# Retention's values computed in the value stage, for all heads at once and kept in DRAM, instead of in a unit of each pair

## What is computed

```
h = rmsnorm(x)
qA,kA,vA | qR,kR,vR,gR | gateA,gateB = split(h @ w_in)
y_A = dilated attention(qA, kA, vA) @ w_a          # 24 heads of 64, three dilation groups of 8 heads
ret = retention(qR, kR, vR)                        # 4 heads, keys 128 wide, values 256 wide
y_B = (silu(gR) * ret * rsqrt(mean(ret^2)))  @ w_b
x = x + (sigmoid(gateA) * y_A + sigmoid(gateB) * y_B) @ w_o
x = x + relu(rmsnorm(x) @ w_up)^2 @ w_down
```

## Time and profile before

| | us |
|---|---|
| median of three runs | 1916.44 (1916.28 to 1916.62) |
| profiled execution, its own time | 1916.38 |
| its span, first to last instruction | 1914.6 |
| TensorE busy | 1907.6 |
| VectorE busy | 1132.0 |
| ScalarE busy | 772.1 |
| GpSimd busy | 89.3 |

### The profile page before, as it was taken

How to read it: one execution, slowest core, us unless ns; L and a number is a source line. 1 busy time by engine, 2 the same in 40 slices (tenths; PEclk the granted TensorE clock), 3 DMA queues, 4 the chain that set the end, 5 groups by cost and what they waited for, 6 DMA issues and landing times.

```text
span 1914.6 us, 23788 instructions
## 1 busy us (share of the span) xinstructions
PE 1907.6 (100%) x9664; PEld 1605.9 (84%) x9664; DVE 1132.0 (59%) x1785; ACT 772.1 (40%) x1197; POOL 89.3 (5%) x72
## 2 busy tenths in 40 slices
PE   9999999999999999999999999999999999999999
PEld 8888888888888888888888888888888888888888
DVE  5567786966456545445635576858755565445354
ACT  7344536463223323223352536454632333223232
POOL 0011110200000000000001110201000000000000
PEclk9999999999999999999999999999999999999999
DMA  4532323224333332332324233223243333323322
GB/s 146 170 94 78 93 84 90 83 67 143 100 110 99 99 96 92 94 105 88 110 96 147 89 88 89 83 77 95 67 154 107 99 92 100 98 88 98 100 88 88
DMA packets 211228, 190.83 MB, mean 100 GB/s; under 512 B 12848, under 2 KB 199984, under 8 KB 210352
## 3 DMA queue, kind: packets, MB, share of 16 engines
q1 hardware_dynamic: 210688, 188.97, 32.2%
q10 hardware_dynamic: 432, 0.35, 0.1%
HBM read 182.87 MB, written 6.43 MB: 99 GB/s over the span
## 4 chain that ended last, share of the span: by engine, by line
PE 98%; ACT 1%; DVE 0%; issue 0%; POOL 0%; DVEq 0%; ACTq 0%; POOLq 0%
PE pj L1474 27%; PE pj L1476 27%; PE pj L1475 27%; PE pj L1682 2%; PE pj L1683 2%; PE pj L1684 2%; PE sc L1581 1%; PE pt L1581 1%; PE sc L1609 1%; PE pt L1589 1%; PE yo L1609 1%; PE sc L1589 1%; PE sc L1539 1%; PE pt L1541 1%; PE sc L1541 1%; PE pt L1539 1%
## 5 line engine op out<-in xcount | busy, mean ns | idle before, releaser
L1474 PE MATMUL pj<-h_hi,w_hi 128*128 128x512 f32 x1408 | 553.4, 393 | 0.0
L1476 PE MATMUL pj<-h_hi,w_lo 128*128 128x512 f32 x1408 | 548.4, 389 | 0.0
L1475 PE MATMUL pj<-h_lo,w_hi 128*128 128x512 f32 x1408 | 548.2, 389 | 0.0
L538 ACT CAST w_hi<-w_raw 128x1024 fp32r<-128x1024 f32 x324 | 325.6, 1049 | 341.0 <-PE pj L1476 247.5
L900 DVE TENSOR_TENSOR w_lo<-w_raw,w_hi 128x1024 fp32r<-128x1024 f32 x327 | 395.3, 1248 | 98.1 <-ACT w_hi L538 96.7
L1474 PEld LDWEIGHTS pj<-h_hi,w_hi 128*128 128x128 f32 x1408 | 264.3, 188 | 56.9 <-issue 1.9
L1476 PEld LDWEIGHTS pj<-h_hi,w_lo 128*128 128x128 f32 x1408 | 264.3, 188 | 55.9
L1475 PEld LDWEIGHTS pj<-h_lo,w_hi 128*128 128x128 f32 x1408 | 264.4, 188 | 53.9 <-issue 0.5
L1474 PE MATMUL pj<-z_hi,w_hi 128*128 128x512 f32 (+1 forms) x656 | 252.0, 384 | 0.0
L1476 PE MATMUL pj<-z_hi,w_lo 128*128 128x512 f32 (+1 forms) x656 | 251.8, 384 | 0.0
L1475 PE MATMUL pj<-z_lo,w_hi 128*128 128x512 f32 (+1 forms) x656 | 251.8, 384 | 0.0
(11 more groups left out here) (262 smaller groups left out, 2338.1 us busy)
## 6 DMA issues: line engine op xcount, KB each, us to landing
w_raw<-in_w_in SPq DMA_DIRECT2D x151, 512.0 KB, 4.5
w_raw<-in_w_up SPq DMA_DIRECT2D x64, 512.0 KB, 4.6
w_raw<-in_w_down SPq DMA_DIRECT2D x64, 512.0 KB, 4.2
w_raw<-in_w_b SPq DMA_DIRECT2D x16, 512.0 KB, 3.8
w_raw<-in_w_o SPq DMA_DIRECT2D x16, 512.0 KB, 4.0
x_scratch<-x SPq DMA_DIRECT2D x2, 2048.0 KB, 10.2
x<-row_scratch SPq DMA_DIRECT2D x16, 256.0 KB, 3.8
w_raw<-in_w_a SPq DMA_DIRECT2D x8, 512.0 KB, 3.4
```

Of the source, the lines that this page charges most:

```text
L538: nc.scalar.copy(w_hi[s][:, c], raw[:, c]).then_inc(hi_done, 1)
L1474: nc.tensor.matmul(out, w_hi[s][:, wc], acts[0], start=first, stop=False)
L1475: nc.tensor.matmul(out, w_hi[s][:, wc], acts[1], start=False, stop=False)
L1476: return nc.tensor.matmul(out, w_lo[s][:, wc], acts[0], start=False, stop=last)
```

## The change

Retention's values leave the pairs. The value stage has five groups: vA group 0, then two groups with the 512 columns of two retention heads each (`VR_AT = (1, 2)`, with h in normal token order), then vA groups 1 and 2. ScalarE writes their high part (`vR_high`) and VectorE their low part into `vT_hi`, `vT_lo`, `vT_last`; SyncE writes these to DRAM (`vR_away`) and reads one head back in each pair (`vR_back`). A pair has five units (0 to 2, 3, and the gate as unit 4). The small matmuls keep their places relative to the unit before them, so that more of them now stand inside units of the next pair (`pair_rest`). The order on ScalarE and VectorE is rewritten for this. The gates of quarter 1 are split: A1 goes ahead of the first w_b unit (`GATES`), with a second buffer `sA1`.

```diff
-    V_U, P_U, G_U, O_U, M_U = 2, 6, 4, 2, 8
+    V_U, P_U, G_U, O_U, M_U = 2, 5, 4, 2, 8
+    VG = 5
+    VR_AT = (1, 2)
+    V_GROUP = (0, None, None, 1, 2)
+    GATES = [("A", 0), ("B", 0), ("A", 1), ("Z", 0), ("Y", 0), ("B", 1), ("Z", 1), ("Y", 1)]
+    GATES += [(k, p) for p in (2, 3) for k in "ABZY"]
...
+                def vR_away(r):
+                    sp.wait_ge(v_out, (l * VG + VR_AT[r] + 2) * TB)
+                    h2 = slice(2 * r, 2 * r + 2)
+                    sp.dma_start(vr_hi_scratch[:, h2], vT_hi[:].bitcast(F32).rearrange("p e b c -> p e (b c)")).then_inc(vr_sent, 16)
...
+                def vR_back(i):
+                    J = l * PAIRS + i
+                    sp.wait_ge(vr_sent, (l + 1) * 96)
+                    sp.wait_ge(rstd_all_done, 2 * l + 1)
+                    sp.wait_ge(ret_mm, 2 * J + 2)
+                    sp.dma_start(vR_hi[:].bitcast(F32).rearrange("p b c -> p (b c)"), vr_hi_scratch[:, i]).then_inc(vr_in, 16)
...
                 value_weights(2)
+                vR_away(0)
+                value_weights(3)
+                vR_away(1)
+                value_weights(4)
                 x_out()
...
+                def vR_high(r):
+                    act.wait_ge(rstd_done, l + 1)
+                    if r == 1:
+                        act.wait_ge(vr_sent, (2 * l + 1) * 48)
+                    for b in range(TB - 1):
+                        act.wait_ge(v_done, (l * VG + VR_AT[r]) * (TB - 1) + b + 1)
+                        nc.scalar.activation(vT_hi[:, :, b, :],
...
                         if g == 0:
                             pe.wait_ge(h_ready, l * 2 * KT + k + 1)
-                        elif g == 1:
+                        elif g == 3:
                             pe.wait_ge(res_done, l * KT + k + 1)
...
-                        for o in range(2):
-                            pe.wait_ge(bank_free[o], l * LQ + i * P_U + 5 + BANK_CREDIT)
+                        pe.wait_ge(vr_in, (J + 1) * 48)
...
                 g0 = l * LU + G0
                 last = l * PAIRS + PAIRS - 1
-                gate(0, 0, 0)
+                gate("B", 0, 0)
                 split_z(range(0, 6))
-                gate(0, 0, 1)
+                gate("B", 0, 1)
                 ret_inverse(last)
-                lo(g0 + 2, 0)
-                gate(0, 1, 0)
+                lo(g0 + 3, 1)
                 ret_scale(PAIRS - 1, 0)
                 ret_scale(PAIRS - 1, 1)
                 split_z(range(6, 8))
-                gate(0, 1, 1)
+                gate("A", 1, 0)
                 y_sum(PAIRS - 1)
-                lo(g0 + 3, 1)
+                gate("A", 1, 1)
+                lo(g0 + 4, 0)
```

More of the change, by code:

```diff
@@ L1001, in _ @@
                 rms_diag(l)
-                for g in range(GROUPS):
+                for g in range(VG):
                     if g > 0:
@@ L1500, in unit @@
                         weights(n)
-                    tile_half(s, o, acts, range(kt), kt, first if o == 0 else None)
-                    if behind[o]:
-                        behind[o]()
+                    for ks in (range(0, 4), range(4, 8))[:kt // 4]:
+                        tile_half(s, o, acts, ks, kt, first if o == 0 else None)
+                        if behind:
+                            behind(o, ks[0] // 4)
             h = (h_hi, h_lo)
@@ L1663, in attend @@
                     q = l * LQ + i * P_U
[L1664 removed]
+                    for s in range(8):
                         u, o, half = 3 + s // 4, s // 2 % 2, s % 2
[L1666 to L1669 removed]
+                        if s in (0, 4):
+                            weights(n + u, 0)
+                        if s in (2, 5):
                             weights(n + u, 1)
@@ L1711, in pair_mean, with pair_rest @@
-                def pair_mean(J):
-                    ret_ones(J)
-                    share_rows(J)
+                def pair_rest(i, u, o, half):
+                    J = l * PAIRS + i
+                    if (u, o, half) == (0, 0, 0):
+                        st(i, 1)
+                        scores(J, 2)
+                        scores(J, 3)
+                    if (u, o, half) == (0, 0, 1):
+                        st(i, 2)
+                        st(i, 3)
+                    if (u, o, half) == (0, 1, 1):
+                        turn(J, 2)
+                        turn(J, 3)
+                        ret(i, 0)
+                    if (u, o, half) == (1, 0, 1):
+                        ret(i, 1)
+                        values(i, 0)
+                        values(i, 1)
+                    if (u, o, half) == (1, 1, 1):
+                        ret_ones(J)
+                        share_rows(J)
@@ L1730, in _ @@
-                last = l * PAIRS + PAIRS - 1
-                gates(0, (lambda: pair_end(PAIRS - 1), lambda: pair_mean(last)))
-                for p in range(1, 4):
-                    gates(p)
+                for j, (kind, p) in enumerate(GATES):
+                    n, q = l * LU + G0 + j, l * LQ + G0 - P0 + j
+                    if kind in "AB":
+                        unit(n, q, n % 2, h,
+                             behind=(lambda o, half: pair_rest(PAIRS - 1, j, o, half)) if j < 2 else None)
+                    elif kind == "Z":
+                        unit(n, q, n % 2, (z_hi, z_lo), KT, lambda k: pe.wait_ge(split_done, l * KT + k + 1))
+                    else:
+                        unit(n, q, n % 2, (y_hi, y_lo), KA, lambda k: pe.wait_ge(y_ready, l * PAIRS + k + 1))
```

378 lines of the change are left out of this document (183 added, 195 removed).

## The result

| | before, us | changed, us |
|---|---|---|
| median of the runs | 1916.36 (1916.08 to 1916.62, 4 runs) | 1942.50 (1940.97 to 1942.72, 4 runs) |
| profiled execution's span | 1914.6 | 1939.2 |
| matmuls | 9664 | 9280 |
| TensorE busy | 1907.6 | 1912.9 |
| mean granted clock | 1.000 | 0.995 |

The ratio is 1.0135, interval 1.0122 to 1.0147: slower, as forecast (1934.0, range 1924 to 1939), but 8.5 us more than forecast and outside the range.

What follows compares the result with a forecast made beforehand. TensorE was taken to bound the kernel, busy 1907.6 of 1914.6 us. Sum: 1916.4 - 4.9 - 0.5 + 15.6 + 7.6 = 1934.2, called 1934, range 1924 to 1939.

Steps and rivals of the forecast that it cites:

- The gains: TensorE: 768 matmuls of 256 columns replaced by 384 of 512, gain 4.9 us; layer 1's wait for the copy gone, 0.5.
- the rule of the Trainium skill that I weighed: Matmul issue: columns divided by 2.4 GHz plus about 2.5 ns; by it the gain would be 1.0 us.
- The 1.0 us wait for weights in layer 1: Start of layer 1, second value group: TensorE's 1.0 us wait for weights was forecast to stay.
- The pairs' wait: Pairs 1 to 3, mostly ahead of turn(1): TensorE waits 2.6 us for VectorE's chain, six times, loss 15.6 us.
- VectorE's share of the chain: Pairs 1 to 3, from the sum matmul through VectorE's rotations, scalings and y_sum: 21.2 us, within a chain of 36.7.
- the moment at which TensorE is ready for `st(0)`: Pairs 1 to 3: TensorE comes to retention's scores 34.1 us after the sum matmul, 45.42 before.
- The 1.1 us by which GpSimd stretches `y_sum`: Pairs 1 to 3: GpSimd's multiplication beside y_sum costs VectorE 1.1 us; without it the loss is 9.0 instead of 15.6.
- The w_b wait: First w_b unit of each layer: gate bank read moved behind a wait, TensorE loses 3.8 us, twice, 7.6 in all.
- DRAM traffic at no cost: Value stage and pairs: SyncE's writes and read-backs cost 0, at most some 4 us per write if loads came late.
- After the wait everything is as far from TensorE as before, so nothing adds up: Behind each wait in the pairs: no further loss, and the next pair waits anew, 3 pairs x 2 layers.

Runs made afterwards that it cites:

- e3_both: Changed kernel with VectorE's gate bank read put back ahead of the scalings of z and y_sum moved behind the next pair's last st_low: 1910.4 us, ratio 0.9969.
- e5_fill_waits: Changed kernel with unneeded 512-column matmuls in place of TensorE's waits (nine and two in pairs 1 to 3, sixteen ahead of w_b): 1934.2 us, ratio 1.0094.
- e4_before_gate_late: Kernel before, with only VectorE's gate bank read moved behind both scalings and the last two splits of z: 1928.5 us, ratio 1.0066.

## Why the prediction was wrong, point by point

**The gains, right.** 4.9 + 0.5 forecast, 1916.3 - 1910.4 = 5.9 measured. A value group of layer 2 (as the earlier trace rows):

```profile
1057.87 0.39 PE L1598 MATMUL sc<-w_hi,res_hi 128*128 128x512 f32 x1
...
1079.41 0.40 PE L1600 MATMUL pt<-w_hi,res_lo 128*128 128x512 f32 x1
```

95 steps in 21.54 us, 0.2267 each. By the rule of the Trainium skill that I weighed ("TensorE: Matmul & The Clock Gate", section "Back-to-back issue gap"), the gain of the matmuls would have been 1.0; the measured total decides for the rows' 4.9. The 1.0 us wait for weights in layer 1, which I let stand, went as well, so the total hides a term that was off: the span fell by 1914.6 - 1908.5 = 6.1, and without the 1.5 of the two waits of the earlier trace rows, and with the 0.3 of the new wait at the start, 4.9 are left for the matmuls.

**The pairs' wait, right.** 2.6 forecast, 2.6 measured, at `turn(1)` and a little at `st(0)`, three per layer and the same each time. VectorE's share of the chain, from the sum matmul (290.37) to the end of the last rotation, was forecast at 21.2; the row that follows it starts at

```profile
311.62 2.35 DVE L948 TENSOR_TENSOR w_lo<-w_raw,w_hi 128x1024 fp32r<-128x1024 f32 x2
```

which is 21.25. The other side, the moment at which TensorE is ready for `st(0)`, was forecast at 34.1 and is 34.11 in `e3_both`. The 1.1 us by which GpSimd stretches `y_sum` were read off another instruction and measured here.

**The w_b wait, right.** 3.8 forecast, 3.77 measured.

**DRAM traffic at no cost, right.** `e3_both` has all of it and no wait. The three writes of a group land in 3.2 to 6.0 us, the head's three reads in 5.6 to 6.6, by their medians (from the full list of the changed kernel's DMA issues: KB each, median us to landing):

```profile
vr_hi_scratch<-vT_hi SPq DMA_DIRECT2D x4, 768.0 KB, 3.2
vr_last_scratch<-vT_last SPq DMA_DIRECT2D x4, 256.0 KB, 6.0
vR_hi<-vr_hi_scratch SPq DMA_DIRECT2D x8, 384.0 KB, 5.6
vR_last<-vr_last_scratch SPq DMA_DIRECT2D x8, 128.0 KB, 6.6
```

**The step that failed: the sum took a wait to cost its own length.** "After the wait everything is as far from TensorE as before, so nothing adds up" is true of the other engines and not of TensorE's clock. The kernel before runs at 1.000 throughout and I took that as given for a kernel into which I had just put eight standstills. They brought 8.8 us (`e5_fill_waits`: 8.3). In the profiled execution, whose own time is 1941.0, they were less: the distances between sum matmuls exceed 74.58 by 1.15 in layer 1 and by 1.42 and 1.21 in layer 2, and at w_b seven matmuls take 3.08 and 3.05 instead of 1.72 (as in layer 2 of `e4_before_gate_late`), 1.36 and 1.33: 6.5 together. Every other term was within 0.2 us but the wait for weights that I let stand (1.0, against 0.3 to 1.0 of new waits at the start). With the clock kept up by filling, the kernel takes 1934.2 against 1934.2 in my sum; that this agrees to the tenth is luck, since gains 0.5 us larger than forecast are offset by 0.5 that the filled places take beyond the waits. The rows of before offered no price for a fall, since it had none in pairs and gates; half pace after a standstill should have been bounded, from nothing to a few us for each, and would have moved the upper end.

## What to carry to other kernels

A wait on a TensorE that is otherwise never idle cost its length here and then, often, one to three us lost at half pace: eight waits of 2.9 us on average cost 4.0 each. Before reordering such a kernel, list each hand-over's room, and after it, look at busy time as well as waits: fewer matmuls and more busy time than the waits' own few tenths points to the clock, and the granted clock by slices shows where. Where a wait can't be taken out of the way, matmuls that nobody needs were cheaper than standing still (8.3 and 4.5 us here); better is to move out of the chain whatever isn't needed at its end, as `y_sum` was.

## What the runs showed of the hardware that I had not expected

- The clock fell to 1.2 GHz behind waits of only 2.0 us listed (2.6 in all), in half of the cases, and the same wait at the same place of the same program was followed by a fall in one layer and not in the other.
- A fall lasted from 4 to 14 matmuls of 512 columns at 0.43 us, not counting the transposes ahead of some. A kernel with such waits is less repeatable: 4.3 us between the runs of `e4_before_gate_late`, 0.9 with the same delay filled.
- By the medians the effects weren't additive: 5.5 us from the two kinds of wait apart, 7.7 together. With runs up to 3.9 us apart within a kernel this isn't settled, and its cause is open.
